# A modulation matrix-vector product taken off TensorE: products on ScalarE, additions on VectorE, partition sums on TensorE

## The reference, cut to what matters

```python
def swiglu(x, w_gate, w_up, w_down):
    return (jax.nn.silu(x @ w_gate) * (x @ w_up)) @ w_down

for l in range(DEPTH):                       # first block, DEPTH = 2
    h = h + 0.5 * swiglu(rmsnorm(h, ffn1_norm[l]), ffn1_w_gate[l], ffn1_w_up[l], ffn1_w_down[l])
    ...                                      # mixer: h @ w_in, retention, attention, w_out
    h = h + 0.5 * swiglu(rmsnorm(h, ffn2_norm[l]), ffn2_w_gate[l], ffn2_w_up[l], ffn2_w_down[l])

# second block, before anything of it:
sh1, sc1, g1, sh2, sc2, g2 = jnp.split((jax.nn.silu(c) @ w_mod + b_mod)[:, None, :], 6, axis=-1)
mod_c = jnp.split(jax.nn.silu(c_ctx) @ w_mod[:, :n_mod * d] + b_mod[:n_mod * d], n_mod)   # n_mod = 2
```

## Time and profile before

| | |
|---|---|
| median of 3 runs | 1750.3 us |
| profiled execution | 1750.12 us, span 1748.3 us |
| TensorE busy | 1729.7 us, 99% of the span |
| VectorE, ScalarE, GpSimd busy | 52%, 40%, 10% |
| granted TensorE clock, mean | 0.998 |
| feed-forward part 0, gate and up | about 6 to 145 us |
| mixer 0 | about 213 to 345 us |
| feed-forward parts 1 and 2, mixer 1, part 3 | up to about 1104 us |
| second block, then its experts | from 1104 us; experts from about 1290 us |

### The profile page before, as it was taken

How to read it: one execution, slowest core, us unless ns; L and a number is a source line. 1 busy time by engine, 2 the same in 40 slices (tenths; PEclk the granted TensorE clock), 3 DMA queues, 4 the chain that set the end, 5 groups by cost and what they waited for, 6 DMA issues and landing times.

```text
span 1748.3 us, 30291 instructions
## 1 busy us (share of the span) xinstructions
PE 1729.7 (99%) x12581; PEld 1415.8 (81%) x12582; DVE 908.9 (52%) x1570; ACT 701.2 (40%) x1179; POOL 166.2 (10%) x173
## 2 busy tenths in 40 slices
PE   9999999999999999999999999999999999999998
PEld 8999988999999999998899999677774445444443
DVE  6655577676655766567678666466731111111111
ACT  6444545464344543454445445454631111111111
POOL 1000042210000100014214000100410000000000
PEclk9999999999999999999999999999999999999999
DMA  9545464545444445557556455232199999999997
GB/s 381 198 173 182 156 250 168 208 169 172 178 181 169 169 173 180 179 169 241 194 192 226 172 192 189 89 85 73 75 421 405 429 427 428 428 428 430 427 428 312
DMA packets 78815, 425.89 MB, mean 244 GB/s; under 512 B 16352, under 2 KB 32992, under 8 KB 41824
## 3 DMA queue, kind: packets, MB, share of 16 engines
q1 hardware_dynamic: 78256, 421.01, 62.7%
q10 hardware_dynamic: 432, 3.10, 0.4%
HBM read 423.03 MB, written 1.05 MB: 243 GB/s over the span
## 4 chain that ended last, share of the span: by engine, by line
PE 90%; DMA 6%; ACT 2%; DVE 2%; issue 1%; POOL 0%; POOLq 0%; SPq 0%; DVEq 0%; ACTq 0%
PE ps L721 18%; PE ps L723 18%; PE ps L722 18%; PE ps L1373 10%; PE ps L1424 5%; DMA ring<-stream_expert 5%; PE ps L1347 3%; PE ps L1049 2%; PE ps L1043 2%; PE ps L1055 2%; PE ps L815 1%; PE ps L1354 1%; ACT w_split L1486 1%; PE ps L1355 1%; DVE w_split L1939 1%
## 5 line engine op out<-in xcount | busy, mean ns | idle before, releaser
L1939 DVE TENSOR_TENSOR w_split<-ring,w_split 128x1024 fp32r<-128x1024 f32 x335 | 425.0, 1276 | 334.1 <-ACT w_split L1486 333.5
L721 PE MATMUL ps<-x_hi,w_split 128*128 128x272 f32 (+1 forms) x1856 | 541.1, 292 | 2.1 <-DVE x_lo L1944 1.7
L723 PE MATMUL ps<-x_hi,w_split 128*128 128x272 f32 (+1 forms) x1856 | 534.0, 288 | 0.0
L722 PE MATMUL ps<-x_lo,w_split 128*128 128x272 f32 (+1 forms) x1856 | 532.1, 287 | 0.0
L1486 ACT ACTIVATE w_split<-ring 128x1024 fp32r<-128x1024 f32 x335 | 350.6, 1054 | 354.4 <-PE ps L723 353.2
L721 PEld LDWEIGHTS ps<-x_hi,w_split 128*128 128x128 f32 x1856 | 350.4, 189 | 14.6 <-issue 9.6
L722 PEld LDWEIGHTS ps<-x_lo,w_split 128*128 128x128 f32 x1856 | 350.4, 189 | 0.3
L723 PEld LDWEIGHTS ps<-x_hi,w_split 128*128 128x128 f32 x1856 | 350.3, 189 | 0.0
L723 PE MATMUL ps<-hid_hi,w_split 128*128 128x272 f32 (+1 forms) x704 | 201.6, 286 | 0.0
L722 PE MATMUL ps<-hid_lo,w_split 128*128 128x272 f32 (+1 forms) x704 | 201.5, 286 | 0.0
L721 PE MATMUL ps<-hid_hi,w_split 128*128 128x272 f32 (+1 forms) x704 | 201.1, 286 | 0.0
(11 more groups left out here) (427 smaller groups left out, 2212.5 us busy)
## 6 DMA issues: line engine op xcount, KB each, us to landing
ring<-stream_ffn SPq DMA_DIRECT2D x131, 1024.0 KB, 4.8
ring<-stream_expert SPq DMA_DIRECT2D x48, 2048.0 KB, 25.0
ring<-stream_expert SPq DMA_DIRECT2D x36, 1024.0 KB, 12.8
arena<-stream_expert SPq DMA_DIRECT2D x16, 2048.0 KB, 25.5
ring<-stream_in SPq DMA_DIRECT2D x27, 1024.0 KB, 4.9
ring<-stream_mod SPq DMA_DIRECT2D x24, 1024.0 KB, 6.9
con<-stream_expert SPq DMA_DIRECT2D x8, 2048.0 KB, 26.1
ring<-stream_out SPq DMA_DIRECT2D x12, 1024.0 KB, 4.9
```

The costliest lines, as they stand in the source:

```text
L721: pe.matmul(to, w[:, 0, k], hi, start=first, stop=False)
L722: pe.matmul(to, w[:, 0, k], lo, start=False, stop=False)
L723: return pe.matmul(to, w[:, 1, k], hi, start=False, stop=last_)
L1939: nc.vector.tensor_tensor(w[:, 1], half_of(n), w[:, 0].bitcast(fp32), ALU.subtract).then_inc(split_ready, 1)
```

## The change

The products with `w_mod` leave TensorE. Its 24 slots become 32 units (q, v): slot q times `silu(c)` (v = 0), and for the first 8 slots also times `silu(c_ctx)` (v = 1). In the feed-forward parts 0 to 2 ScalarE multiplies a slot's 8 chunks of 256 columns by a per-partition value, four in one step and four in the next (`mod_products`); VectorE adds the 8 products to one row of 256 columns in three additions two steps behind the unit's first (`mod_add`). The sum over the 128 partitions is made by TensorE for two units together (a portion p): four products with a stationary operand that has a single column of ones (`mod_portion`), 13 of the 16 portions in gate and up steps, most of them six steps behind their second unit, and three in mixers. VectorE adds the result to `mod_row` (`mod_collect`). The batches are two instead of three.

The units stand at steps 3, 5, ... 17 of part 0, at 1, 3, ... 15 of parts 1 and 2 (`MOD_EARLY`), and at down halves 1, 6, 11, 16 of parts 1 and 2 (`MOD_LATE`). The modulation slot for a unit at step j is filled behind feed-forward slot j + 1. A slot with v = 1 is in use for two units; its place in the ring is free when VectorE has added the second.

```diff
-    for q in range(IN_SLOTS):
-        FILLS += [("in", _l, q)] + ([("mod", _l * MOD_MIX + q - 1)] if 1 <= q < 1 + MOD_MIX else [])
+    FILLS += ffn_fills(2 * _l)
+    FILLS += [("in", _l, q) for q in range(IN_SLOTS)]
...
+MOD_UNITS = [(q, v) for q in range(8) for v in range(2)] + [(q, 0) for q in range(8, MOD_SLOTS)]
+MOD_EARLY = [(3, 5, 7, 9, 11, 13, 15, 17), (1, 3, 5, 7, 9, 11, 13, 15), (1, 3, 5, 7, 9, 11, 13, 15), ()]
+MOD_LATE = [(), (1, 6, 11, 16), (1, 6, 11, 16), ()]
+MOD_BUFFERS = 3
+PORTIONS = [{11: 0, 15: 1, 19: 2}, {9: 4, 13: 5, 17: 6, 21: 7}, {1: 8, 2: 9, 9: 10, 13: 11, 17: 12, 21: 13}, {}]
+MIXER_PORTIONS, PORTIONS_AT = [(3,), (14, 15)], 8
...
                     elif before[0] == "mod":
-                        sp.wait_ge(raw_done, RAW_AT[before] + 1)
+                        sp.wait_ge(mod_summed, LAST_UNIT[before] + 1)
...
+            def mod_portion(p, bank, col=T):
...
+                pe.wait_ge(mod_summed, 2 * p + 2)
...
+                for i in range(2):
+                    for j in range(2):
+                        own, at = 2 * n + j, 64 * i + 32 * j
+                        last = pe.matmul(ps[at:at + 32, bank, col:col + P], unit_row[:, 32 - own:64 - own], mod_sums[:, p % MOD_BUFFERS, j, i * P:i * P + P],
+                                         start=True, stop=True)
+                last.then_inc(mod_used, 1)
...
-                    if x % 2 == 1 and 0 <= (x - 3) // 2 < MOD_MIX:
-                        mod_rows(l * MOD_MIX + (x - 3) // 2)
...
+                def mod_products(u, half):
...
+                    to = mod_product if q < 8 and v == 0 else w
+                    if half == 0:
+                        act.wait_ge(slot_full[m % NS], full_count(m))
...
+                    for c in range(4 * half, 4 * half + 4):
+                        last = nc.scalar.activation(to[:, c], w[:, c], ACT.Identity, scale=cc[:, c, v:v + 1])
+                    if half == 1:
+                        last.then_inc(mod_scaled, 1)
...
+                def mod_add(u):
...
+                    dve.wait_ge(mod_scaled, u + 1)
+                    nc.vector.tensor_tensor(part[:, 0:4], part[:, 0:4], part[:, 4:8], ALU.add)
+                    dve.drain()
+                    nc.vector.tensor_tensor(part[:, 0:2], part[:, 0:2], part[:, 2:4], ALU.add)
+                    dve.drain()
+                    if u % 2 == 0 and p >= MOD_BUFFERS:
+                        dve.wait_ge(mod_used, p - MOD_BUFFERS + 1)
+                    nc.vector.tensor_tensor(mod_sums[:, p % MOD_BUFFERS, u % 2], part[:, 0], part[:, 1], ALU.add).then_inc(mod_summed, 1)
...
                 for j in range(F):
...
+                    if j - 2 in units:
+                        mod_add(units[j - 2])
```

More of the change, by code:

```diff
@@ L33 @@
 OUT_FILLS = OUT_SLOTS // 2
-MOD_SLOTS, MOD_MIX = 24, 11
+MOD_SLOTS = 24
 MOD_COLS = SLOT // C
@@ L47, with mod_units, ffn_fills @@
 LAST_TILE = {"zf": "zf1", "zb": "zb1", "zv": "zvc"}
[L48 removed]
 WARM = 3
 MOD_TURN_AT = 25
+MOD_UNITS = [(q, v) for q in range(8) for v in range(2)] + [(q, 0) for q in range(8, MOD_SLOTS)]
+MOD_FFN = [range(0, 8), range(8, 20), range(20, 32), range(0)]
+MOD_EARLY = [(3, 5, 7, 9, 11, 13, 15, 17), (1, 3, 5, 7, 9, 11, 13, 15), (1, 3, 5, 7, 9, 11, 13, 15), ()]
[3 more added lines that the diff above has]
+MIXER_PORTIONS, PORTIONS_AT = [(3,), (14, 15)], 8
+MOD_FIRST = [0, 4]
+def mod_units(f, early):
+    n = len(MOD_EARLY[f])
+    return dict(zip(MOD_EARLY[f], MOD_FFN[f][:n])) if early else dict(zip(MOD_LATE[f], MOD_FFN[f][n:]))
+def ffn_fills(f):
+    behind = {j + 1: MOD_UNITS[u] for j, u in mod_units(f, True).items()}
+    behind.update({GU_SLOTS + (i + 3) // 2: MOD_UNITS[u] for i, u in mod_units(f, False).items()})
+    fills = []
+    for s in range(FFN_SLOTS):
+        fills.append(("ffn", f, s))
+        if s in behind and behind[s][1] == 0:
+            fills.append(("mod", behind[s][0]))
+    return fills
 FILLS = []
 for _l in range(DEPTH):
[L55 to L57 removed]
+    FILLS += ffn_fills(2 * _l)
+    FILLS += [("in", _l, q) for q in range(IN_SLOTS)]
     FILLS += [("out", _l, s) for s in range(OUT_FILLS)]
[L59 to L60 removed]
+    FILLS += ffn_fills(2 * _l + 1)
 FILLS += [("in2", name) for name in IN2] + [("out2", r) for r in range(OUT_SLOTS // 2)]
@@ L402, in build @@
         MOD_AT = 64
-        m = layout(small, MOD_AT, [("mod", 48, 2), ("a1", C, 2), ("a2", C), ("cc", C, 64), ("ss", 8), ("vstd", 8), ("vr", 8),])
-        mod_row = cut(arena, ARENA - MOD_COLS, MOD_COLS)
-        mod, a1, a2, cc, v_ss, v_std, v_rstd = (m[x] for x in ("mod", "a1", "a2", "cc", "ss", "vstd", "vr"))
+        m = layout(small, MOD_AT, [("mod", 48, 2), ("a1", C, 2), ("a2", C), ("cc", C, 2), ("unit", 64), ("ss", 8), ("vstd", 8), ("vr", 8),])
+        mod_row = cut(arena, ARENA - P, P)
+        mod, a1, a2, cc, unit_row, v_ss, v_std, v_rstd = (m[x] for x in ("mod", "a1", "a2", "cc", "unit", "ss", "vstd", "vr"))
+        mod_product = cut(arena, rest + (F + 4 + 2 * HID_SPLITS) * T, C, MOD_COLS)
+        mod_sums = cut(ring, X_AT, MOD_BUFFERS, 2, MOD_COLS)
+        assert rest + (F + 4 + 2 * HID_SPLITS) * T + SLOT <= ARENA - P and MOD_BUFFERS * 2 * MOD_COLS <= 3 * 512
         SH1, SC1, G1, SH2, SC2, G2 = (slice(C * i, C * i + C) for i in range(6))
@@ L1559, in ffn @@
                         hidden_hi(j - 2)
+                    for half in range(2):
+                        if j - half in units:
+                            mod_products(units[j - half], half)
+                units = mod_units(f, False)
                 for i in range(F - 2):
@@ L1563, in ffn @@
                         hidden_hi(i + HID_SPLITS)
+                    for half in range(2):
+                        if i - half in units:
+                            mod_products(units[i - half], half)
                     if f == 2 * DEPTH - 1 and i == 4:
```

97 lines of the change are left out of this document (55 added, 42 removed).

## The result

The kernel after takes 1775.99 us (median of 4 runs, 1774.4 to 1777.1), the one before 1750.57 on the same chip: a ratio of 1.0144, 95% interval 1.0132 to 1.0155. It is slower, by 25.4 us where 15 were forecast, and lies 1 us above the range. The profiled execution has a span of 1774.4 us against 1748.3.

The account below looks back on a forecast made before the run. TensorE, busy 99% of the span, was taken as the bound. Work removed and added gave -14.0 us, six ring waits +28.3, portions hidden in them -2.5, slow clock +3.4: +15.2 on 1750.1, so 1765.3 us, range 1738 to 1775.

Parts of the forecast that it names:

- mixers, removed less given back: Two mixers: 22 product groups of 1.19 us leave TensorE, 26.2 us, of which 6.4 come back as waits.
- portions: TensorE: sixteen portions of four half-wide products at 0.5 us each add 8.0 us.
- first stop of each part: First two feed-forward parts: slots 10 and 8 are refilled late, and TensorE idles 2.1 us at each.
- four further stops, with the slow clock they absorb: Later two-unit slots pay the whole latency: 6.2 and 5.5, then 6.9 and 5.5 us; portions falling into waits save 2.5.
- the lag at the first stop: VectorE's lag grows 0.1 to 0.4 us a step, reaching 0.65 us four steps after the first unit.
- Slots, queue, landing, engine times: Six waits in SyncE's in-order queue; 4.8 us from issue to landing; ScalarE 1.65 us a step, VectorE 2.45 a unit.
- The last such slots: Slots 23 and 21 of the first two feed-forward parts cause no wait, being released two steps ahead.
- The clock: TensorE's clock drops after idling, losing 1.7 us; only behind each part's last wait does it count, 3.4 us or nothing.
- The removed work: TensorE's modulation products in the mixers: 1.19 us a group; waits at tiles 7, 9 and scores return 3.2 a mixer.
- Nothing in part 2: Third feed-forward part: each slot serves one unit, so its copy is some 0.3 us late against a lead of 6.
- the first (the slot comes in time): Rival: ring slots are refilled in time, so only the removed work counts: -14.0 us, 1736 us; chance 20%.
- The third, that the pace is the bound: Rival: ScalarE's activations take 2.1 us, making a step 6.6; some 6 to 10 us more, 1773 us; chance 8%.

Follow-up runs that it names:

- the first experiment: Kernel after with each modulation slot in the feed-forward parts filled behind feed-forward slot j + 2 instead of j + 1: 1739.36 us, ratio 0.9938 to the kernel before.
- The experiment with later units: Kernel after with the units of parts 0 and 1 moved to steps 5, 7, ... 19 and their portions behind them: 1772.82 us, ratio 1.0123 to before.
- the experiment with two stops: Kernel after with slots filled behind j + 2, except the first of part 0 and second of part 1, kept at j + 1: 1754.45 us, ratio 1.0023.
- third: Kernel after with one 1024-column activation in place of four of 256 in each half unit, mostly with wrong factors: 1766.84 us, ratio 1.0091 to before.
- sixth experiments: Kernel after with slots filled behind j + 2 and VectorE's additions three steps behind a unit instead of two: 1773.17 us, ratio 1.0133 to before.

## Why the prediction was wrong in size and right in mechanism

| term | forecast | measured |
|---|---|---|
| mixers, removed less given back | -19.8 | -16.5 |
| second block | -2.2 | -1.5 |
| portions | +8.0 | +7.2 |
| first stop of each part | 2 x 2.1 | 5.1 + 5.7 |
| four further stops, with the slow clock they absorb | 24.1 - 2.5 | 21.3 |
| slow clock behind the last stop of each part | +3.4 | +3.1 |
| slot 23 of part 0, at the first down half | 0 | +1.7 |
| sum | +15.2 | +26.1 |

Of the 10.9 us between the two sums, the first stops are 6.6, the mixers 3.3 and slot 23 1.7; the other terms take back 0.7. The range missed by 1 us.

**The step that failed** is the lag at the first stop: "the lag grows by about 0.1 to 0.4 a step, to 0.65 us four steps after the first unit". It put the gate of step 7 at 2.23 + 0.65 = 2.9 us behind the end of half 15; it was 5.7: half 15 ended on TensorE where half 16 starts, at 59.96 in this row, and the gate is the row at 65.65 above.

```profile
59.96 0.29 PE L742 MATMUL ps<-x_hi,w_split 128*128 128x272 f32 x1
```

I had read the lag off a steady step far into a part, but VectorE enters every part 11 to 13.5 us behind TensorE. In the kernel before a step of ScalarE and VectorE takes 4.48 us against 6.05, and the lag falls to 2.5 within five steps. The change starts its units at step 3 or 1, and from there a step takes as long as TensorE's: the lag stays where it then is. It drains only slowly once the hidden parts are done, in the first experiment from 5.9 us at step 9 to 3.7 at step 20. Gate against the end of the half in part 0, steps 3 to 7: 5.4, 3.8, 2.5, 2.5, 2.5 us before, 5.4, 5.4, 5.4, 5.7, 5.7 after. With 2.8 us more of lag the forecast of 2.1 becomes 4.9, and the trace has 4.91. In part 1 the lag is 6.0 and the transfer took 5.2 us where 4.8 was counted: 2.1 + 3.1 + 0.4 = 5.6, and the trace has 5.57. The experiment with later units shows it from the other side: lag 2.5 to 2.9 us, first stops of 1.98 and 1.86. The prediction had itself written that the two "can't catch up", and didn't ask from what.

**Slots, queue, landing, engine times**: right. The places of all six stops, 4.86 us from issue to copy (4.8), 1.70 and 2.5 us of work (1.65, 2.45). The loop from stop to stop also held: from one stop's first product to the next's are 30.26, 29.51, 31.04 and 29.60 us, against 30.4, 29.7, 31.1 and 29.7. Slow clock and stop together are 5.5, 4.7, 6.3 and 4.8 us, against 24.1 - 2.5 for the four. (The 2.5 counts five portions between the stops; the program has four there, at steps 11 and 15 of part 0 and 9 and 13 of part 1, so it should be 2.0.) The prediction set these apart from the first stops and was right that they don't hang on the lag at the start.

**The last such slots**: wrong. The prediction left out slots 23 and 21 because they are "released two steps ahead". By the count of steps they are, but in part 0 ScalarE wanted slot 23 only 3.1 us behind the additions and waited 1.70 us, which reached TensorE in full.

**The clock**: right that it falls behind each stop, and nearly in its size: 1.7 forecast, 1.4 to 1.6 here. That the next stop absorbs it is borne out by the loops, which only then have the forecast length. But the experiment with two stops, 2.3 and 2.5, and the one with later additions, 2.4 to 2.6 behind three of its six, show that 1.7 is no upper bound.

**The removed work**: 3.3 us too much. The give-back in mixer 0 was 3.3 us in all against 3.2, though other tiles share it: 1.0 at tile 7, 0.8 at 9, 0.6 at 13 and at 25, and small ones; in mixer 1 it was 4.0, with 1.1 at tile 13. The mixers are shorter by 8.5 and 8.0 us where 10 each were forecast. But a group was worth 1.07 us on average, not 1.19; beside attention's own small products, behind tiles 15 and on, the tiles came only 0.87 to 1.0 us earlier a group, and the earlier trace rows was a group between long ones.

**Nothing in part 2**, and no wait for the sums: right; only its six portions show there, 0.55 us each. Of the rivals, the first (the slot comes in time) had the price of the mended version nearly right, 1736 against 1739.4, but not for this change. The third, that the pace is the bound, named 1773 and so came nearest in time. The first, third and sixth experiments show that its mechanism is not at work.

## What to carry to other kernels

When a buffer of a ring gets a second, slower user, count from the end of that user to the step that wants the next content of its place, and compare with the transfer's time from issue to landing plus the lag of that moment; a step more of distance in the fill order may cost nothing and decide everything (one number was worth 36.6 us here, with 0.1 us to spare at the first slot). Do this for every such slot, the last ones too, where the engines' steps get shorter. Read the lag where the new work begins, not in the steady state: added work that fills an engine's slack keeps whatever lag it finds for many steps. Before work is taken off an engine for its length, look for the waits that it covers; and small work can be put into them.

## What the runs showed of the hardware

- **Short stops are dearer than their idle time.** Idle times of TensorE of 3.0 to 5.6 us were followed by a granted clock of 0.50 that went on while TensorE had work again, 1.4 to 1.6 us lost in the kernel after and 2.3 to 2.5 in the one with two stops, where its rows at 0.50 begin earlier, while TensorE still stands, and end later (76 to 82 us against 77 to 80). The Trainium skill (TensorE: Matmul & The Clock Gate, "Part 1: The HAM clock gate") gives the same two levels and says that idling brings the engine back to the lower one; these rows agree. After the 1.98 us of idle time in the experiment with later units the clock stayed at 1.00:

```profile
84.00:86.00 2.00, 0.70 (x6) 0.48 (x4) 0.70 (x1) 1.79 (x2) 0.00 (x0) 1.00 1.01 430
86.00:88.00 2.00, 1.32 (x10) 1.35 (x11) 2.00 (x4) 0.22 (x1) 0.00 (x0) 1.00 1.01 426
88.00:90.00 2.00, 2.00 (x18) 2.00 (x17) 0.81 (x3) 1.95 (x6) 0.00 (x0) 1.00 1.02 430
```

  One of 2.14 us in the experiment with short products did have a slow clock behind it, and so did the one of 2.02 us in the experiment with later additions: the idle time alone doesn't tell.
- **A small product between long ones isn't cheap.** One of four columns cost 0.36 us where a group of eight of 256 columns cost 1.19, and a portion of four half-wide products 0.45 to 0.55 us.
- **One wide activation against four narrow ones**: 1.14 us for 1024 columns with a per-partition factor, 1.70 us for four of 256.
